# A two-block transformer on one core: its compression stage on column groups of the array, and its changes of stage in units of two feature tiles

## The reference, cut to what matters

```
u = rms_norm(h, norm_mix_pre)                 # every stage begins so
q, kc, vc, ks, vs, kw, vw, g, ... = split(u @ w_in)
kc = gelu(flat(blocks(kc) + pos) @ cmp_w1_k) @ cmp_w2_k      # 15 blocks of 32 tokens, 2 groups; the same for vc
gates = sigmoid(g)                            # 24 columns
h = h + rms_norm(y @ w_out, post); u = rms_norm(h, mlp_pre)
f = square(relu(u @ w_mlp_in)) @ w_mlp_out
u = rms_norm(h, g) * (1 + scale) + shift      # second block, scale and shift from silu(c) @ ada_w + ada_b
f = (silu(u @ wi[:, :F]) * (u @ wi[:, F:])) @ wo
```

## Time and profile before

| what | us |
|---|---|
| three runs | 1342.6, 1342.3, 1341.03 |
| median | 1342.3 |
| the profiled execution | 1341.63 |
| its span in the trace | 1339.6 |
| TensorE busy | 1302.0 |
| DVE busy | 930.4 |
| ACT busy | 661.5 |

### The profile page before, as it was taken

One profiled execution on the slowest core, in us unless ns is written; L12 is line 12 of the kernel. 1 busy time (PEld: TensorE's weight loads), 2 busy tenths in 40 slices (PEclk: granted clock), 3 DMA queues, 4 the chain that ended last, 5 costly groups with the idle time before them and its releaser, 6 DMA issues.

```text
span 1339.6 us, 16194 instructions
## 1 busy us (share of the span) xinstructions
PE 1302.0 (97%) x6503; PEld 1070.1 (80%) x6503; DVE 930.4 (69%) x1029; ACT 661.5 (49%) x928; POOL 28.3 (2%) x56
## 2 busy tenths in 40 slices
PE   8998998999999999999999999999999999999998
PEld 8986676888887788887788887787888887788887
DVE  5368888776658776677876667966766786744444
ACT  5355765645456444445544445753344566644442
POOL 2200010000000000000000000000000000000000
PEclk9999998999999999999999999999999999999999
DMA  8996668777775787874678784587778632455551
GB/s 252 259 364 193 189 236 322 273 286 278 274 290 205 260 293 280 281 279 147 240 262 281 281 311 163 183 300 278 257 279 280 224 126 97 156 188 188 189 188 63
DMA packets 162762, 317.98 MB, mean 237 GB/s; under 512 B 7128, under 2 KB 108944, under 8 KB 153472
## 3 DMA queue, kind: packets, MB, share of 16 engines
q1 hardware_dynamic: 158800, 305.44, 65.9%
q0 software_dynamic: 3712, 11.45, 3.2%
q10 hardware_dynamic: 176, 0.05, 0.0%
HBM read 314.56 MB, written 1.84 MB: 236 GB/s over the span
## 4 chain that ended last, share of the span: by engine, by line
PE 87%; DVE 8%; ACT 3%; issue 1%; DMA 1%; SPq 0%; ACTq 0%; DVEq 0%
PE bank L736 27%; PE bank L738 26%; PE bank L737 26%; PE bank L847 2%; DVE full L1978 2%; DVE wlo L1869 1%; DVE xt L1966 1%; DVE mix L1964 1%; ACT whi L1390 1%; DMA raw<-in_w_in 1%; PE bank L773 1%; PE bank L797 0%; PE bank L1105 0%; DVE mix L1978 0%; DMA xt<-in_x 0%
## 5 line engine op out<-in xcount | busy, mean ns | idle before, releaser
L1869 DVE TENSOR_TENSOR wlo<-raw,whi 128x2048 fp32r<-128x2048 f32 x202 | 462.5, 2291 | 222.3 <-ACT whi L1390 222.1
L1390 ACT ACTIVATE whi<-raw 128x2048 fp32r<-128x2048 f32 x205 | 392.2, 1914 | 179.1 <-PE bank L738 169.2
L736 PE MATMUL bank<-whi,uhi 128*128 128x512 f32 (+2 forms) x1168 | 454.9, 389 | 11.3 <-DVE ulo L1991 7.4
L738 PE MATMUL bank<-whi,ulo 128*128 128x512 f32 (+2 forms) x1168 | 446.3, 382 | 0.0
L737 PE MATMUL bank<-wlo,uhi 128*128 128x512 f32 (+2 forms) x1168 | 445.4, 381 | 0.0
L736 PEld LDWEIGHTS bank<-whi,uhi 128*128 128x128 f32 x1168 | 220.7, 189 | 58.4 <-issue 17.4
L738 PEld LDWEIGHTS bank<-whi,ulo 128*128 128x128 f32 x1168 | 220.6, 189 | 43.2
L737 PEld LDWEIGHTS bank<-wlo,uhi 128*128 128x128 f32 x1168 | 221.0, 189 | 40.0 <-issue 0.5
L736 PE MATMUL bank<-whi,hsplit 128*128 128x512 f32 (+1 forms) x512 | 198.0, 387 | 0.0
L738 PE MATMUL bank<-whi,hsplit 128*128 128x512 f32 (+1 forms) x512 | 195.9, 383 | 0.0
L737 PE MATMUL bank<-wlo,hsplit 128*128 128x512 f32 (+1 forms) x512 | 195.8, 382 | 0.0
(11 more groups left out here) (269 smaller groups left out, 928.8 us busy)
## 6 DMA issues: line engine op xcount, KB each, us to landing
raw<-in_ffn_w_in SPq DMA_DIRECT2D x176, 512.0 KB, 4.7
ada<-in_ada_w SPq DMA_DIRECT2D x72, 1024.0 KB, 7.5
raw<-in_ffn_w_out SPq DMA_DIRECT2D x44, 1024.0 KB, 5.0
raw<-in_w_in SPq DMA_DIRECT2D x16, 1024.0 KB, 8.1
raw<-in_w_mlp_in SPq DMA_DIRECT2D x16, 1024.0 KB, 6.8
raw<-in_w_mlp_out SPq DMA_DIRECT2D x16, 1024.0 KB, 4.8
ada<-in_kv_ada_w SPq DMA_DIRECT2D x8, 1024.0 KB, 7.5
raw<-in_w_kv SPq DMA_DIRECT2D x8, 1024.0 KB, 5.1
```

Source lines behind the costliest of these rows:

```text
L736: nc.tensor.matmul(o, sh, mh, start=start, stop=False, skip_group_check=skip)
L738: return nc.tensor.matmul(o, sl, mh, start=False, stop=stop, skip_group_check=skip)
L1390: ins = nc.scalar.activation(whi[:, ring(n), :], raw[:, ring(n), :], ACT.Copy)
L1869: ins = nc.vector.tensor_tensor(wlo[:, ring(n), :], raw[:, ring(n), :], whi[:, ring(n), :].bitcast(F32), ALU.subtract)
```

## The change

- **Values.** `k_and_v` becomes `keys`, `values` and `values_of_two`: slots 5 and 6 (swapped in what they hold) give their values in products of 256 columns that take both slots' columns. `pe_done` rises by two at its end.
- **Compression.** Stage `cmp` leaves the ring: the 4 MB of cmp_w1 are loaded unsplit into `ada` (keys, issued before slot 5) and `wide` (values, before slot 7). 16 fp32 products of 32 output rows and 256 columns for each, the products 0, 1, 2, 3 going to partitions 0, 32, 64, 96 of the bank and so on round; the gates are 8 products of that form. ACT copies the four partial sums (`gate_parts`, `h_parts`), and small products with `four` (four identities of 32 over each other) add and turn them. GELU comes behind that. Slot G + 3 is run before the turning of the compressed probabilities. The first two of the jobs wait for `cmp_mm`.
- **Jobs and pieces.** The five jobs of the front are gone from there, five more lie in mlp (slots 5, 9, 13, 17, 21). Pieces move as in `WINDOW` and `PIECES_AT` below; in the pool stage `keep_busy` takes their place.
- **Changes of stage.** `first_chunk` works in units of two tiles, eight of them, in the order c, t, half. ACT makes `full` of the even units and `uhi` of all, DVE `full` of the odd units and `ulo` of all. For t = 0 (not e = 1) a unit is an fp32 product of x with the identity scaled by the root; t = 1 is turned as before. For e = 1 x is turned without its root, and the root is the scale of the ReLU. The first part of a root (the mean of the first half) is formed between the squares. DVE splits slot n + 1 in halves between the units; ACT splits slot n + 2 after the last unit (for e = 1 before unit 6).

```diff
@@ schedule
-for _s, _c in ((START["cmp"] + 2, 1), (START["gate"], 1), (START["gate"] + 2, 1), (START["gate"] + 3, 1),
-               (START["gate"] + 5, 1)):
-    JOBS_AT[_s] = tuple(next(_jobs) for _ in range(_c))
...
 for _n in ("mlp", "ffn0", "ffn1", "ffn2"):
-    for _m in list(range(2, 32, 2)) + [31]:
+    _odd = [5, 9, 13, 17, 21, 31] if _n == "mlp" else [31]
+    for _m in sorted(list(range(2, 32, 2)) + _odd):
...
-                        ((1, 1), (((0, 1), "turn", 7, 0), (2, 0, 4, 0), (2, 1, 5, 0), (3, 0, 6, 0))),
-                        (("mlp", 3), ((3, 1, 7, 0),)),
-                        ((2, 0), ((4, 0, 6, 0), (4, 1, 7, 0))),
-                        ((2, 1), ((5, 0, 4, 0), (5, 1, 5, 0))),
+                        (("mlp", 3), (((0, 1), "turn", 7, 0),)),
+                        (("mlp", 10), ((2, 0, 7, 0),)),
+                        (("mlp", 12), ((2, 1, 7, 0),)),
+                        (("mlp", 14), ((3, 0, 7, 0),)),
+                        (("mlp", 16), ((3, 1, 7, 0),)),
+                        ((2, 0), ((5, 0, 4, 0), (5, 1, 5, 0), (4, 0, 6, 0), (4, 1, 7, 0))),
...
-                        ((3, 0), (((18, 19), "sum", 7, 0),)),
-                        ((3, 1), (((18, 19), "turn", 7, 0),)),
-                        ((4, 0), ((8, 0, 4, 0),)),
-                        ((4, 1), ((8, 1, 5, 0),)),
+                        (("ffn0", 20), (((18, 19), "sum", 7, 0),)),
+                        (("ffn0", 22), (((18, 19), "turn", 7, 0),)),
+                        ((4, 0), ((8, 0, 7, 0),)),
+                        ((4, 1), ((8, 1, 6, 0),)),
...
-                        ((5, 0), (((9, 10), "sum", 7, 0),)),
-                        ((5, 1), (((9, 10), "turn", 7, 0),)),
-                        (("ffn2", 4), ((11, 0, 7, 0),)),
-                        (("ffn2", 6), ((11, 1, 7, 0),)),
-                        (("ffn2", 8), (((12,), "sum", 7, 0),)),
-                        (("ffn2", 10), (((12,), "turn", 7, 0),)),
-                        ((6, 0), ((13, None, 7, 0), ((15, 16), "sum", 6, 0))),
-                        ((6, 1), (((15, 16), "turn", 6, 0), (14, 0, 4, 0), (14, 1, 5, 0)))):
+                        (("ffn1", 20), (((9, 10), "sum", 7, 0),)),
+                        (("ffn1", 22), (((9, 10), "turn", 7, 0),)),
+                        ((5, 0), ((11, 0, 7, 0), (11, 1, 6, 0))),
+                        (("ffn2", 4), (((12,), "sum", 7, 0),)),
+                        (("ffn2", 6), (((12,), "turn", 7, 0),)),
+                        (("ffn2", 20), (((13,), "sum", 7, 0),)),
+                        (("ffn2", 22), (((13,), "turn", 7, 0),)),
+                        ((6, 0), ((14, 0, 4, 0), (14, 1, 5, 0))),
+                        ((6, 1), (((15, 16), "sum", 6, 0),)),
+                        (("wq", 2), (((15, 16), "turn", 7, 0),))):
@@ TensorE, the front
+            def values_of_two():
+
+                wh, wl = (w[:, 0:3:2, :].rearrange("p s (k c) -> p s k c", k=8)[:, :, :, P:2 * P] for w in (whi, wlo))
+                for t in range(2):
+                    for k in range(KT):
+                        ins = mm3(bank[5 * (1 - t)][:, T:2 * T], uhi[:, k, tokens(t)], ulo[:, k, tokens(t)], wh[:, :, k, :],
+                                  wl[:, :, k, :], k == 0, k == KT - 1)
+                ins.then_inc(pe_done, 2)
...
+            for k in range(KT):
+                c = 32 * (k % 4)
+                ins = nc.tensor.matmul(bank[6][c:c + 32, 0:T], wgs[:, 24 * k:24 * k + 32], full[:, k, :], start=k < 4,
+                                       stop=k >= 4, skip_group_check=True)
...
             for a in range(2):
+                pe.wait_ge(w1_in[a], 32)
+                pe.wait_ge(blk_full, 2)
                 for ii in range(16):
+                    c, at = 32 * (ii % 4), 480 * a + 30 * ii
+                    ins = nc.tensor.matmul(bank[4 + a][c:c + 32, 0:T], mix[:, at:at + 32],
+                                           w1s[a][ii // 8][:, T * (ii % 8):T * (ii % 8 + 1)], start=ii < 4, stop=ii >= 12,
+                                           skip_group_check=True)
+                ins.then_inc(cmp_mm, 1)
...
+            for a in range(2):
+                pe.wait_ge(h_copied, a + 1)
+                for m in range(2):
+                    ins = nc.tensor.matmul(bank[7][:, 32 * (2 * a + m):32 * (2 * a + m) + 30],
+                                           h_parts[a][:, m * P:(m + 1) * P], four[:, 0:30], start=True, stop=True)
@@ TensorE, a change of stage
+                for k in range(2):
+                    to, s = unit_bank(e, i)[:, k * P:(k + 1) * P], slice((kk + k) * P, (kk + k + 1) * P)
+                    if e == 1:
+                        ins = nc.tensor.transpose(to, xt[:, t, s], ident)
+                    elif t == 0:
+                        ins = nc.tensor.matmul(to, xt[:, 0, s], mix_t[:, 0, 0:P], start=True, stop=True)
+                    else:
+                        ins = nc.tensor.transpose(to, mix_t[:, t, s], ident)
...
+            BUSY = {1: (0, 8), 2: (0, 0), 4: (0, 4), 5: (0, 0), 6: (0, 0), 7: (8, 4)}
...
+                window(e, 0)
+                keep_busy(before_turn, spare)
+                turn_unit(e, 0)
+                turn_unit(e, 1)
+                window(e, 1)
+                keep_busy(behind, spare)
...
+                part(0, 0, 2)
+                turn_unit(e, 2)
+                turn_unit(e, 3)
+                part(0, 0, 3)
+                pe.wait_ge(u_lo, first + 2)
+                part(1, 0, 0)
+                part(1, 0, 1)
+                turn_unit(e, 4)
+                pe.wait_ge(u_lo, first + 3)
+                part(1, 0, 2)
+                turn_unit(e, 5)
+                part(1, 0, 3).then_inc(pe_done, 1)
...
+                part(0, 1, 0)
+                part(0, 1, 1)
+                turn_unit(e, 6)
+                pe.wait_ge(u_lo, first + 5)
+                part(0, 1, 2)
+                turn_unit(e, 7)
+                part(0, 1, 3)
+                pe.wait_ge(u_lo, first + 6)
+                part(1, 1, 0)
+                part(1, 1, 1)
+                pe.wait_ge(u_lo, first + 7)
+                part(1, 1, 2)
+                part(1, 1, 3).then_inc(pe_done, 1)
@@ ACT
+            def normed_u(v, g, shift, silu=False):
+
+                squares(v, 0, 0)
+                squares(v, 0, 1)
+                link(root(0, 0))
+                nc.scalar.activation(mix_t[:, 0, 0:P], ident, ACT.Copy, scale=cell(0, 3)).then_inc(u0_ready, 1)
+                squares(v, 1, 0)
+                full_unit(v, 0, g, shift)
+                high_unit(v, 0)
+                squares(v, 1, 1)
+                high_unit(v, 1)
+                link(root(1, 0))
+                scaled(0)
+                full_unit(v, 2, g, shift)
...
+                full_unit(v, 6, g, shift)
+                high_unit(v, 6)
+                high_unit(v, 7)
+
+            def turn(v, n, g, shift, normed=False, silu=False):
+
+                conv(n + 1)
+                if normed:
+                    for t in range(2):
+                        for c in range(2):
+                            post_half(v, t, c)
+                normed_u(v, g, shift, silu)
                 conv(n + 2)
@@ DVE
+            def made_u(v, n, g, shift):
+
+                full_unit(v, 1, g, shift, (0,))
+                low_unit(v, 0)
+                full_unit(v, 1, g, shift, (1,))
+                low_unit(v, 1)
+                if v == 2:
+                    take_sums(WINDOW[2, 0][:2])
+                else:
+                    conv_half(n + 1, 0)
+                full_unit(v, 3, g, shift)
+                low_unit(v, 2)
+                low_unit(v, 3)
...
+                full_unit(v, 7, g, shift)
+                low_unit(v, 6)
+                low_unit(v, 7)
```

453 lines of the change are left out of this document (251 added, 202 removed).

## The result

The median after is 1354.05 us (1348.81 to 1354.73, 4 runs), before 1342.01: ratio 1.0079, interval 1.006 to 1.0098: 0.8% slower, clear of the noise. The forecast was 1333.9, range 1319 to 1342. The profiled execution has a span of 1352.3 us, 12.7 more than before, and that difference is followed here.

The account below looks back on a forecast made before the run. TensorE, 97% busy, was taken as the bound. Front -9.9, e = 1 -6.2, five other changes +6.0, pieces +5.9, pool -1.0 gave -5.2 (1337); halves taken back made it -8.4, so 1333.9 us, range 1319 to 1342.

Parts of the forecast that it names:

- Values of two slots: Front: 96 products of 128 columns become 48 of 256, 4.8 us less on TensorE's path.
- Compression and gates: Front: unsplit fp32 products in four column groups, 0.5 us a round; stage 14.6 to 7.0 us, 7.6 less.
- Rival D: Quarters do not overlap when each has its own weights: 17 us instead of 5, 1346 us in all; chance 0.03.
- What is late next there: DMA: Front: 4.2 MB of weights issued earlier make slot 10 land at 73, costing 3.5 us; bounds 0 and 9.
- Behind it: Front's end: slot G+3 covers a 2.06 us wait and lost clock, about 2.5 bare before first gate part; net -1.0.
- e = 1: Change of stage out to mlp: products start sooner after x is turned without its root; 6.2 us less, bounds -8 and -3.
- rival E: e = 1 runs at half clock because of idle time: +4 us, 1338 us in all; chance 0.07.
- The five other changes: Changes of stage 2, 4, 5, 6, 7: earlier starts -11.3, new waits and work more; +6.0, +4.5 after half-backs.
- third slot: Five other changes: ACT splits slot n+2 only after the last unit, a new wait taken as 1.2 us each, bounds 0 and 2.
- Rival C: Third-slot and unit waits at full price, DVE's queue adding: five changes +18 instead of +4.5, 1347 us; chance 0.10.
- Pieces: Pieces moved: mlp +3.0, ffn0 and ffn1 +2.8, ffn2 -0.3, wq +0.4; +5.9 us.
- Pool: Pool stage: one DVE copy leaves the path (0.7), 14 transposes end 0.8 late; -1.0 us, bounds -2 and +1.

Follow-up runs that it names:

- values_apart: bias_late with the values of slots 5 and 6 in products of 128 columns each again, instead of both in one of 256: 1332.80 us, ratio 0.993.
- bias_late: Kernel before with the changed front alone, and GpSimd sending bias rows and reading tables once slot 10 has landed instead of slot 6: 1328.17 us, ratio 0.9903.
- third_early: Changed kernel, but in the five other changes ACT splits slot n+2 ahead of unit 6 instead of behind unit 7: 1347.03 us, ratio 1.0042.
- dve_order: Changed kernel with late tables, early third-slot split and second gates, units 4 and 6 turned and low parts made earlier, DVE reordered in e = 5, 6: 1336.58 us.
- gates_first: bias_late with ACT splitting slot 10 behind its copies of the gate and compression sums instead of ahead of them: 1330.37 us, ratio 0.9914.
- e1_units: bias_late with e = 1 alone done in units, the five other changes of stage as before: 1326.98 us, ratio 0.9891.

## Why the prediction was wrong

- **Values of two slots, -4.8: right** (4.7 in the trace of values_apart), once no transfer hid it.
- **Compression and gates, -7.6: right and a little low.** Rounds took 0.43 us instead of 0.5, and in bias_late the stage runs from 64.19 to 70.00, 5.8 us for the 7.0 of the forecast. Rival D is out.
- **"What is late next there: DMA", +3.5, half of it taken back: the step that failed in the front.** By 73.33 the changed kernel was 4.5 us behind before instead of 4.8 ahead: transfers cost 9.3 us up to there (6.92 of wait, 2.2 of half clock) and 1.88 more at the gate sums, 11.2 in all for a forecast of 1.8 and an upper bound of 9. The step added up megabytes at the page's mean rate, had TensorE wait only behind slot 10, and had no term for the clock behind a wait. What the runs show in its place: from 45 to 55 us the DMA engines move 200 instead of 378 GB/s because of the bias rows; with 4.2 MB more ahead of slot 7 this fell on a slot that was needed. Taking half of it back "where engines run ahead" had no row behind it.
- **Behind it, -1.0: measured 0.** 2.3 us ahead at 81.10 and 2.3 ahead at the end; the bare wait of "about 2.5" behind `in_taken` is there (2.21), and half clock behind this wait and at the start of slot G (0.74 in 110 to 115, 0.67 in 80 to 85). In bias_late, at full clock in both places, the same part gains 1.9 (13.4 ahead at slot G, 15.3 at the end).
- **e = 1, -6.2: right in mechanism**, -5.0 measured. The first product came 3.47 us behind the last (3.0 forecast), and the third slot 14.8 behind the first product (13.9 forecast), by the waits for units; the third slot itself is not waited for. Products ran at 0.23 us from the start (granted clock 1.00 in 224 to 229), so the clock held, against rival E; that is the place where the forecast set the trace against the Trainium skill (TensorE: Matmul & The Clock Gate, PE-mode transpose), and the trace was right for so short a stretch.
- **The five other changes, +4.5: measured +15.1 with wq's piece. The second step that failed.** The starts came earlier by 10.5 (11.3 forecast). The third slot was priced well (1.2 forecast; 1.23 to 1.40 idle, and third_early gained 5 to 7 us over five).
  - Mis-sized was the hand-off of a unit, taken as 1.3 us against 0.68 of products: turned at 1159.31, unit 2 was used at 1161.50, 2.2 us later, since the working left out DVE's low part (0.42) and the steps from one engine to the next. Units 4 and 6 have two parts to cover them, 1.36 us of products and not 0.68, and were late all the same: their low part stands on DVE behind the making of the next unit. The waits for units 2, 4 and 6 are 0.90, 0.55 and 0.45 idle; by the distances of starts beyond 0.23 they are 1.07, 0.71 and 0.62, 2.4 per change instead of 1.2.
  - In e = 2 the wait for the third slot did not go away (1.32 us) but changed its cause. And e = 6 has a wait of 1.91 us for the rotated queries that the prediction does not name: half pieces moved behind the change on DVE's queue.
  - In sum, beyond the 6.4 us worked out (with wq's piece, before anything was taken back): unit waits 6.0, rotated queries 1.9, the wait of e = 2 some 1.3, the third slot about 1, later starts 0.8; against it about 2.0 for a wait of the kernel before that the working did not credit (0.23 to 0.26 idle in each change, ahead of its second half).
  - Rival C named the right place and sign at 0.10; its "from 2.8 us per change on" was just passed (2.9 to 3.0), which with the other terms as forecast would have given 1344, 2 us above before; the front's 9.3 did most of the rest.
- **Pieces, +5.9: near** (3.1 in mlp and 3.3 in the three ffn, 6.4 for 5.5; wq's 0.4 lies in a wait of e = 6). Pool -1.0, measured -1.5; five jobs more in mlp cost nothing.

The forecast stood at 1342.3 - 8.4, the trace at 1342.3 + 12.7. Of these 21.1 us the front has 9.3, the five changes 10.2 (15.1 for 4.9 with wq's piece), e = 1 1.2, pieces and pool 0.4. The sum also took "one half of each" back, but of the 2.4 us per change it took 0.3, where half is 1.2; done as said it would have been further off. And the range ended at 1342, below rivals C (1347) and D (1346), which had 0.13 between them. One of its own signs of being wrong came true: ACT waited 3.41 us for slot 10.

## What to carry to other kernels

When a change brings loads forward, list every user of the DMA engines in that stretch with its rate, also those that other engines issue for later; moving the one that can wait can be worth more than the arithmetic saved (here 12 us), and where it may stand depends on where the queue has a hole. When work is cut into finer units, count the whole chain of a unit (turn, make, high, low, and the wait of each queue for its other duties) against the products that cover it; in this kernel, swapping two short instructions in such a chain moved the wait on, and what gave time back was the place of a long operation (the split of a slot, third_early and dve_order). A move that is good in one version can cost as much in the other: the late tables cost 13 us in the kernel before and gave 12 in the changed front.

## What was not expected of the hardware

- DMA engines at a busy share of 0.93 to 1.11 moved 187 to 213 GB/s with the bias rows and 369 to 386 without; the share alone does not tell how much a queue can still take.
- After 3.30 us of idle time the granted clock stayed at 1.00 (bias_late), after 3.08 it was 0.50 in the next five microseconds (gates_first), with the same instructions around it: the starts of 12 products lie within 2.62 us and within 4.86. Whether an idle time of this length costs the clock could not be read from its length. The Trainium skill (TensorE: Matmul & The Clock Gate, Part 1: The HAM clock gate) also calls the number of slow products run-variable; the rows, one execution of each kernel, show 0 and 12.
- The end of the front differs by 5.5 us between kernels that are the same up to there (208.05 in bias_late, 213.56 in e1_units), with a wait for slot 7 of nothing or 1.28 us, one for a gate part of 3.30 or 4.62 and the clock behind it. Why it does so is left open; it is why e1_units shows only 1.2 of its 4.8 us.
